# A two-block transformer kernel: second Fourier transform for 129 of 256 positions and the rest mirrored, one reciprocal per attention job, a double norm by one root

## What is computed

```python
def diff_attend(q, k, v, lam):
    s = jnp.einsum("bqhcd,bkhcd->bhcqk", q, k).astype(jnp.float32) * (HEAD_DIM ** -0.5)
    p = jax.nn.softmax(s, axis=-1)
    a = p[:, :, 0] - lam * p[:, :, 1]
    return jnp.einsum("bhqk,bkhe->bqhe", a.astype(v.dtype), v)

def fourier_mix(f):
    B, S = f.shape[:2]
    fg = f.reshape(B, S, N_FGROUPS, FGROUP_DIM).astype(jnp.float32)
    y = jnp.fft.fft2(fg, axes=(1, 3), norm="ortho").real
    return y.reshape(B, S, FOURIER_WIDTH).astype(f.dtype)

def rms_norm(x, g):
    xf = x.astype(jnp.float32)
    y = xf * lax.rsqrt(jnp.mean(xf * xf, axis=-1, keepdims=True) + EPS)
    return (y * g.astype(jnp.float32)).astype(x.dtype)
```

## Time and profile before

| | us |
|---|---|
| median of 3 runs | 2753.19 (2752.36 to 2753.29) |
| profiled execution, whole | 2750.1 |
| its span, first to last instruction | 2748.3 |
| TensorE busy | 2636.5 (96%) |
| VectorE busy | 1593.8 (58%) |
| ScalarE busy | 976.0 (36%) |
| mean granted TensorE clock | 0.977 of full |

### The profile page before, as it was taken

One profiled execution on the slowest core, in us unless ns is written; L12 is line 12 of the kernel. 1 busy time (PEld: TensorE's weight loads), 2 busy tenths in 40 slices (PEclk: granted clock), 3 DMA queues, 4 the chain that ended last, 5 costly groups with the idle time before them and its releaser, 6 DMA issues.

```text
span 2748.3 us, 36869 instructions
## 1 busy us (share of the span) xinstructions
PE 2636.5 (96%) x15140; PEld 2169.6 (79%) x15140; DVE 1593.8 (58%) x2895; ACT 976.0 (36%) x1737; POOL 52.5 (2%) x55
## 2 busy tenths in 40 slices
PE   8999999999999999999999999998998989997896
PEld 5888888867889888898888897898997777784442
DVE  4877765285447768558776473766555754444111
ACT  4322233276334222242222343744444523222111
POOL 0000000000000000000000000000000000001220
PEclk9999999999999999999999999999999899998998
DMA  7536452200323455334566332053525122157997
GB/s 312 204 141 245 151 195 90 108 1 31 123 92 123 159 202 198 131 123 169 213 269 252 136 123 92 32 209 125 211 85 204 47 77 93 62 222 312 401 382 301
DMA packets 56823, 456.53 MB, mean 166 GB/s; under 512 B 10704, under 2 KB 21328, under 8 KB 21840
## 3 DMA queue, kind: packets, MB, share of 16 engines
q1 hardware_dynamic: 49456, 446.01, 42.1%
q0 software_dynamic: 6912, 6.32, 0.7%
q10 hardware_dynamic: 288, 1.84, 0.2%
HBM read 497.11 MB, written 1.05 MB: 181 GB/s over the span
## 4 chain that ended last, share of the span: by engine, by line
PE 86%; DMA 5%; DVE 4%; ACT 2%; issue 1%; SPq 0%; POOL 0%; DVEq 0%; ACTq 0%; POOLq 0%
PE ps L516 65%; PE ps L2537 3%; PE ps L1926 3%; PE ps L1421 1%; PE ps L3517 1%; PE ps L3144 1%; PE ps L1398 1%; PE ps L2596 1%; PE ps L521 1%; DMA BIG<-eup 1%; DMA U<-edn 1%; DMA U<-eup,extra_ids 1%; ACT fh L503 1%; PE ps L3543 1%; PE nb L3543 1%
## 5 line engine op out<-in xcount | busy, mean ns | idle before, releaser
L516 PE MATMUL ps<-UL,fh 128*128 128x512 f32 (+1 forms) x2096 | 732.5, 349 | 11.4 <-DVE UL L867 5.3
L510 DVE TENSOR_TENSOR fl<-wr,fh 128x1024 fp32r<-128x1024 f32 (+2 forms) x436 | 481.9, 1107 | 446.5 <-ACT fh L503 445.7
L516 PE MATMUL ps<-UH,fl 128*128 128x512 f32 (+1 forms) x2096 | 729.8, 348 | 0.0
L516 PE MATMUL ps<-UH,fh 128*128 128x512 f32 (+1 forms) x2096 | 729.6, 348 | 0.0
L503 ACT CAST fh<-wr 128x1024 fp32r<-128x1024 f32 (+2 forms) x436 | 414.3, 954 | 319.3 <-PE ps L516 298.5
L516 PEld LDWEIGHTS ps<-UL,fh 128*128 128x128 f32 x2096 | 398.3, 190 | 65.3 <-DVE UL L867 6.0
L516 PEld LDWEIGHTS ps<-UH,fl 128*128 128x128 f32 x2096 | 398.5, 190 | 49.5
L516 PEld LDWEIGHTS ps<-UH,fh 128*128 128x128 f32 x2096 | 398.3, 190 | 49.6
L564 DVE SCALAR_TENSOR_TENSOR acc<-wr,CA 128x1024 f32<-128x1024 f32 x256 | 312.4, 1220 | 3.7
L516 PE MATMUL ps<-HL,fh 128*128 128x512 f32 (+1 forms) x770 | 267.4, 347 | 0.0
L516 PE MATMUL ps<-HH,fl 128*128 128x512 f32 (+1 forms) x770 | 266.9, 347 | 0.0
(11 more groups left out here) (565 smaller groups left out, 3542.2 us busy)
## 6 DMA issues: line engine op xcount, KB each, us to landing
wr<-ws SPq DMA_DIRECT2D x135, 2048.0 KB, 8.0
wr<-ws SPq DMA_DIRECT2D x32, 1408.0 KB, 5.9
wr<-eup SPq DMA_DIRECT2D x32, 1024.0 KB, 11.5
BIG<-eup SPq DMA_DIRECT2D x22, 1024.0 KB, 16.2
wr<-edn SPq DMA_DIRECT2D x16, 1024.0 KB, 14.2
wr<-ws SPq DMA_DIRECT2D x11, 1024.0 KB, 7.6
BIG<-edn SPq DMA_DIRECT2D x11, 1024.0 KB, 11.4
X<-eup SPq DMA_DIRECT2D x6, 1024.0 KB, 9.8
```

The source lines that it names most:

```text
L510: e.tensor_tensor(lv, raw_tile(sp.units[n]), hv.bitcast(F32), ALU.subtract).then_inc(*low_done.inc("low", event))
L516: i = e.matmul(out, l, r, start=first and n == 0, stop=last and n == len(pairs) - 1, skip_group_check=True)
```

## The change

In the loops: the transform over positions is made for 129 of 256 positions, the cosine part in the left half of NB and the sine part in the right half. With real output the position 256 − s has the same cosine part as s and the opposite sine part. ScalarE copies the cosine part of 129 positions ("fr even"); VectorE then writes the difference to positions 129 to 255, in reversed order, and the sum to positions 0 to 128 (`mirrored`). It does so at the start of every even job from the third on, and once behind the loop. The event "fr" is now VectorE's.

The two reciprocals of a job (two values for each query block) become one over four values, ahead of both blocks and behind the last exponential of the job. The product with minus lambda is taken into the scaling, as its second scalar.

Where the blocks meet: the sums of squares of both norms are made by matmuls with all-ones matrices, which leave them on every partition, and the factor of the second norm over the first is formed as one inverse root of (sum of the gained squares / D + eps × sum of squares / D + eps²). The inverse roots are a logarithm and an exponential over 256 columns. The root of the first norm, needed for the first block's output, is made by ScalarE behind the eight u.

```diff
@@ -777,13 +777,6 @@
-        def pe_spread(e, name, n, src):
-            e.wait_ge(*at("rms", name))
...
+        def pe_pair_means(e, name, prev):
+            e.wait_ge(*at("scaled", prev[:3], 7))
+            e.wait_ge(*at("square sum", prev, 6))
+            small = eps[:, 0:1].to_broadcast([128, 128])
+            e.matmul(NB[:, 256:512], ones, RS[:, 256:512], start=True, stop=False, skip_group_check=True)
+            e.matmul(NB[:, 256:512], small, RS[:, 0:256], start=False, stop=False, skip_group_check=True)
+            e.wait_ge(*at("square", prev, 7))
+            last = rot.of("stats", prev)
+            e.matmul(NB[:, 256:512], ones, last[:, 256:512], start=False, stop=False, skip_group_check=True)
+            e.matmul(NB[:, 256:512], small, last[:, 0:256], start=False, stop=True, skip_group_check=True).then_inc(
+                *sums.inc("pair sums", name))
+            e.wait_ge(*at("spread", name))
+            e.matmul(NB[:, 0:256], ones, RS[:, 0:256], start=True, stop=False, skip_group_check=True)
+            e.matmul(NB[:, 0:256], ones, last[:, 0:256], start=False, stop=True, skip_group_check=True).then_inc(
+                *sums.inc("stats", prev))
+
         def act_norm_pair(e, name, prev, shift):
-            e.wait_ge(*at("stats", prev))
-            e.activation(root[:, 0:2], NB[:, 0:2], ACT.Sqrt, scale=1.0 / D, bias=eps[:, :]).then_inc(*act.inc("first root", name))
-            e.wait_ge(*at("second square", name))
-            e.activation(root[:, 2:4], root[:, 2:4], ACT.Sqrt, scale=1.0 / D, bias=eps[:, :]).then_inc(*act.inc("root", name))
+            e.wait_ge(*at("pair sums", name))
+            e.wait_ge(*at("eps squared"))
+            e.activation(NB[:, 256:512], NB[:, 256:512], ACT.Ln, scale=1.0 / D, bias=st[:, 57:58]).then_inc(*act.inc())
+            e.wait_ge(*act.now())
+            e.activation(RS[:, 256:512], NB[:, 256:512], ACT.Exp, scale=-0.5).then_inc(*act.inc("spread", name))
             for k in range(8):
                 e.wait_ge(*at("scaled", name, k))
                 e.activation(U[:, k, 0:256], U[:, k, 0:256], ACT.Identity, bias=shift[:, 0, k:k + 1],
                              scale=AB[:, 0, k:k + 1]).then_inc(*act.inc("u", name, k))
+            e.wait_ge(*at("stats", prev))
+            e.activation(NB[:, 0:256], NB[:, 0:256], ACT.Ln, scale=1.0 / D, bias=eps[:, :]).then_inc(*act.inc())
+            e.wait_ge(*act.now())
+            e.activation(NB[:, 0:256], NB[:, 0:256], ACT.Exp, scale=-0.5).then_inc(*act.inc("first spread", name))
 
         def dve_norm_pair(e, name, first_gain, gain, scale):
             dve_gains(e, LAT, gain, scale)
             e.wait_ge(*dve.now())
             e.tensor_tensor(AB[:, 0, :], AB[:, 0, :], first_gain, ALU.mult).then_inc(*dve.inc())
-            e.wait_ge(*at("first root", name))
-            e.reciprocal(rinv[:, 0:2], root[:, 0:2]).then_inc(*dve.inc())
-            e.wait_ge(*dve.now())
-            e.tensor_tensor(root[:, 2:4], NB[:, 2:4], rinv[:, 0:2], ALU.mult).then_inc(*dve.inc())
-            e.wait_ge(*dve.now())
-            e.tensor_tensor(root[:, 2:4], root[:, 2:4], rinv[:, 0:2], ALU.mult).then_inc(*dve.inc("second square", name))
-            e.wait_ge(*at("root", name))
-            e.reciprocal(rinv[:, 2:4], root[:, 2:4]).then_inc(*dve.inc())
-            e.wait_ge(*dve.now())
-            e.tensor_tensor(rinv[:, 2:4], rinv[:, 2:4], rinv[:, 0:2], ALU.mult).then_inc(*dve.inc("rms", name))
             e.wait_ge(*at("spread", name))
             for k in range(8):
-                e.tensor_tensor(U[:, k, 0:256], X[:, k, 0:256], NB[:, 256:512], ALU.mult).then_inc(*dve.inc("scaled", name, k))
+                e.tensor_tensor(U[:, k, 0:256], X[:, k, 0:256], RS[:, 256:512], ALU.mult).then_inc(*dve.inc("scaled", name, k))
 
         def dve_first_block_out(e, first_gain, i):
 
+            if i == 0:
+                e.wait_ge(*at("first spread", "nmix"))
             for k in (2 * i, 2 * i + 1):
...
                 if half:
-                    (act_log_exp if halves else act_root_table)(e)
+                    act_log_exp(e)
...
                     e.wait_ge(*at("f1", l, s, g))
-                    for n, (l_, r_) in enumerate([(r[:, 0:128], cs[:, 0, :]), (r[:, 128:256], ss[:, 0, :]),
-                                                  (r[:, 256:384], cs[:, 1, :]), (r[:, 384:512], ss[:, 1, :])]):
-                        m = e.matmul(NB[:, 0:256], l_, r_, start=n == 0, stop=n == 3, skip_group_check=True)
+                    for x, table in enumerate((cs, ss)):
+                        for tt in range(2):
+                            m = e.matmul(NB[:, 256 * x:256 * x + 129], r[:, 256 * tt + 128 * x:256 * tt + 128 * x + 128],
+                                         table[:, tt, 0:129], start=tt == 0, stop=tt == 1, skip_group_check=True)
                     m.then_inc(*sums.inc("dft2", l, s, g))
...
-                        e.copy(frT[g][:, s * 256:s * 256 + 256], NB[:, 0:256]).then_inc(*act.inc("fr", l, s, g))
+                        e.copy(frT[g][:, s * 256:s * 256 + 129], NB[:, 0:129]).then_inc(*act.inc("fr even", l, s, g))
...
+            def mirrored(i):
+                s, g = divmod(i, 4)
+                f = frT[g][:, s * 256:s * 256 + 256]
+                e.wait_ge(*at("fr even", l, s, g))
+                e.tensor_tensor(f[:, 129:256][:, ::-1], f[:, 1:128], NB[:, 257:384], ALU.subtract).then_inc(*dve.inc())
+                e.wait_ge(*dve.now())
+                e.tensor_tensor(f[:, 0:129], f[:, 0:129], NB[:, 256:385], ALU.add).then_inc(*dve.inc("fr", l, s, g))
+
             for n, (h, s) in enumerate(jobs):
                 if n == len(jobs) - 1:
                     low_parts(e, sp, sp.next_one())
+                if n % 2 == 0 and 0 < n <= 8 * len(segs):
+                    mirrored(n // 2 - 1)
                 klo, khi = keys_of(s)
                 nk = khi - klo
                 for qb in range(2):
@@ -1738,18 +1755,20 @@
                         e.wait_ge(*at("score", l, n, qb, c))
                         e.tensor_reduce(st[:, z + c:z + c + 1], psum.of("p", l, n, qb, c)[:, 0:nk], AX.X, ALU.min).then_inc(
                             *dve.inc("least", l, n, qb, c))
+                zs_ = st[:, 16 + (n % 2) * 16:32 + (n % 2) * 16].rearrange("p (q x) -> p q x", q=2)
+                e.wait_ge(*at("p", l, n, 1, 1))
+                e.reciprocal(zs_[:, :, 2:4], zs_[:, :, 4:6]).then_inc(*dve.inc())
                 for qb in range(2):
                     z = 16 + (n % 2) * 16 + qb * 8
                     p0, p1 = PA[(n % 3) * 2 + qb], PA[6 + qb]
-                    e.wait_ge(*at("p", l, n, qb, 1))
-                    e.reciprocal(st[:, z + 2:z + 4], st[:, z + 4:z + 6]).then_inc(*dve.inc())
-                    e.wait_ge(*dve.now())
-                    e.tensor_tensor(st[:, z + 6:z + 7], st[:, z + 3:z + 4], nlam, ALU.mult).then_inc(*dve.inc())
-                    e.wait_ge(*dve.now())
-                    e.tensor_scalar(p1[:, 0:nk], p1[:, 0:nk], st[:, z + 6:z + 7], None, ALU.mult).then_inc(*dve.inc())
+                    if qb == 0:
+                        e.wait_ge(*dve.now())
+                    e.tensor_scalar(p1[:, 0:nk], p1[:, 0:nk], st[:, z + 3:z + 4], nlam, ALU.mult, ALU.mult).then_inc(*dve.inc())
                     e.wait_ge(*dve.now())
                     e.scalar_tensor_tensor(out=p0[:, 0:nk], in0=p0[:, 0:nk], scalar=st[:, z + 2:z + 3], in1=p1[:, 0:nk],
                                            op0=ALU.mult, op1=ALU.add).then_inc(*dve.inc("a", l, n, qb))
+            if len(jobs) == 8 * len(segs):
+                mirrored(4 * len(segs) - 1)
...
-            pe_stats(e, prev, 512, ("ffn", 1, 1))
-            pe_spread(e, "nmix", 4, rinv)
+            pe_pair_means(e, "nmix", prev)
...
-            e.wait_ge(*at("x", ("ffn", 1, 1, 1), 7))
+            e.memset(st[:, 57:58], EPS * EPS).then_inc(*dve.inc("eps squared"))
```

More of the change, by code:

```diff
@@ L778, in act_inverse_root @@
             e.activation(NB[:, 0:T], NB[:, 0:T], ACT.Exp, scale=-0.5).then_inc(*act.inc("spread", name))
-        def pe_spread(e, name, n, src):
-            e.wait_ge(*at("rms", name))
-            for t in range(n):
-                i = e.matmul(NB[:, t * 128:t * 128 + 128], src[:, t:t + 1].to_broadcast([128, 128]), ident, start=True,
-                             stop=True, skip_group_check=True)
-            i.then_inc(*sums.inc("spread", name))
         def dve_gains(e, segs, gain, scale, ks=slice(0, 8)):
```

## The result

The changed kernel takes 2762.42 us in the median of nine runs (2759.35 to 2767.32); nine runs of the kernel before beside them lie between 2744.06 and 2754.73 around 2753.19. The ratio is 1.0044, with an interval of 1.0033 to 1.0056: slower by 0.44% (the two medians are 9.2 us apart), where 0.57% had been forecast. The profiled execution has a span of 2760.6 us against 2748.3.

What follows compares the result with a forecast made beforehand. TensorE (9.78 us per pair) and a VectorE chain through ScalarE's exponentials bound the loop closely together. 11.45 + 4.1 + 0 = +15.6 us on 2750.1 gave 2765.7, plus 3.1 to the median: 2768.8, range 2762 to 2777.

Steps and rivals of the forecast that it cites:

- One reciprocal per job: Attention loops: joint reciprocal waits for block 2's last exponential; jobs become 6.29 us (512 keys) and 4.36 us (256).
- The mirror: VectorE, ahead of the even job's minima: two additions from PSUM add 0.53 us, bounds 0.45 and 0.72.
- The second scalar: VectorE's attention scaling: a second scalar read from memory adds 0.06 us to each scaling.
- the doubled rate: Rival, attention scaling: a second scalar in memory ends its doubled rate, adding 10.7 us, to 2779.5; chance 7%.
- The transform: Second position transform on TensorE: 129 columns cut it from 1.89 to 1.05 us, relieving 0.84 us per pair.
- First layer's shift: First attention loop: 78.59 us becomes 90.04, +11.45 us, passed on whole to what follows.
- Second layer: Second attention loop: 48.09 us becomes 53.04, +4.95, partly absorbed by TensorE at the end, leaving +4.1 us.
- Double norm: Where the blocks meet: 0 us, since a weight transfer releases TensorE; clock bounds −2.1 and +2.1 us.
- TensorE stays the bound: Rival, loops: VectorE's work fits under TensorE's 8.94 us per pair; 9 us faster, 2744; chance 4%.
- The clock falls: Rival, loops: TensorE's clock falls in thin stretches; once in each of eight pairs +8 us, 2777; chance 12%.
- About the same: Rival, loops: part of the wait overlaps unseen, giving 2748 to 2758 us; chance 6%.
- What would show it: Loop signs: pairs of 11.2 us, second-layer jobs of 6.3, VectorE gaps of 1.2 and some 1 us, scaling 0.55.

Runs made afterwards that it cites:

- The moved wait alone: Kernel before with only VectorE's wait for block 1's exponential put ahead of both query blocks: 2766.52 us, ratio 1.0062.
- the split alone: Kernel after with each query block given its own reciprocal again, behind its own exponential; transform, mirror, second scalar and norm stay: 2738.99 us, ratio 0.9953.
- the second-scalar kernel: Kernel before with only the product with minus lambda taken into the scaling as second scalar, two reciprocals kept: 2745.42 us, ratio 0.9975.
- six old-norm executions: Profiled runs with the old double norm, among them before and after with old norm (2764.98 us): 16.5 us mean from memset to end of gate rows.
- five executions: Profiled runs with the new double norm and the gate weights' load in its old place: 13.2 us mean from memset to end of gate rows.
- The two sets: Kernel after measured twice against the kernel before: 2762.42 us, ratio 1.0044, and again 2758.43 us, ratio 1.0028.
- the one with the joint reciprocal: Kernel before with only the attention reciprocal joined and the product with minus lambda taken into the scaling: 2758.79 us, ratio 1.0036.

## Why the prediction was right, point by point

**One reciprocal per job.** Right in mechanism and size. 3.60 us to the reciprocal of a 512-key job, measured 3.59; jobs of 6.29 and 4.36, measured 6.30 and 4.39; a pair of 11.18, measured 11.21. The moved wait alone reproduces the gaps, and the split alone removes them.

**The mirror** took 0.52 (0.53 forecast), the reversed write at 279 ns no more than a plain one. **The second scalar** costs 0.06 us, as forecast (0.55 and 0.41 us, where the earlier trace rows has 0.49 and 0.35), and the doubled rate is kept: that rival is out. **The transform** went from 1.89 to 1.05 us, as the earlier trace rows had it.

**First layer's shift.** From the first minimum to the last combination 90.22 (90.04 forecast); the gate tile stands at 648.80, 93.95 behind the loop's start at 554.85, where it was 82.45: +11.5. The start of the second loop follows the first by 1156.86 us instead of 1145.37, again +11.5. It was passed on whole.

**Second layer.** To the last combination 52.95 (53.04 forecast). TensorE's last gate-tile work, by the start of ScalarE's first root behind it, is 61.02 behind the loop's start where it was 57.05: +4.0 (+4.1 forecast). The reading that TensorE bounds the jobs of this loop before (it stands in the first rival, which gives four transforms a gain there, and in two expectations) was wrong, as the second-scalar kernel showed; it did not enter the sum, which took the loop's measured length.

**Double norm: the step that failed.** "I take 0", with a lower bound of −2.1 for the clock alone. The prediction read one chain of waits, saw the transfer last, and costed the norm's own chain at nothing because it was covered. But the cover was a tie: in before the norm would have let the gate rows start 6.9 us behind the memset (ScalarE's first u starts at 6.2, and where the norm came last the gate rows start 0.75 us behind that), the transfer at 7.9. In four of the six old-norm executions the order is the other way. And the second round of the old norm's small matmuls already ran at half clock, behind 1.6 us without TensorE work; with the new norm the clock stayed up (stretches, before and after):

```profile
2072.40:2074.48 2.08, 2.08 (x8) 1.78 (x8) 0.00 (x0) 0.00 (x0) 0.00 (x0) 0.50 1.09 378
```

```profile
2083.30:2085.00 1.70, 0.75 (x5) 0.32 (x3) 0.09 (x1) 0.83 (x2) 0.00 (x0) 1.00 0.99 369
```

Measured over five executions the new norm saves 3.3 us; in the profiled execution 4.5, of which 2.1 in the gate rows' clock, my lower bound, and 2.4 in their start.

**The sum.** 2768.8 was forecast and 2762.42 measured: inside the range of 2762 to 2777 by 0.4 us, and 0.4 below the forecast's own 2762.8 to 2773.2. The loops were right to 0.2 us; that the total stayed in the range is in part luck.

15.6 − 3.3 = 12.3 us. The two sets gave 0.44% and 0.28% of some 2752 us: 12.1 and 7.7. The first fits the corrected sum, the second lies 4.6 below, and its interval ends at 10.7. What is left is open.

The two profiled executions differ by 12.3 us in their spans, and that agreement is no proof either: the first loop starts 1.6 us earlier, the two loops' starts are 11.5 further apart, the second block's memset follows 3.2 later, and from there to the end only 0.7 us of the norm's 4.5 is left (679.5 before, 678.8 after). Over the same six and five executions as above that last distance has means of 679.6 and 675.9, so the saving does reach the end in the mean.

One source of such differences can be seen: two executions of the very same program took 666.0 and 659.8 us from the gate rows to the end, with different stretches of half clock. In each of these stretches of 30 us (the first of the kernel after, the second of its repetition, both from 65 us behind the gate rows) the granted clock differs:

```profile
2160.00:2190.00 30.00, 30.00 (x116) 25.62 (x116) 20.38 (x53) 17.69 (x55) 3.51 (x1) 0.58 0.00 1
```

```profile
2160.60:2190.60 30.00, 30.00 (x125) 25.88 (x125) 22.29 (x58) 17.99 (x55) 3.51 (x1) 0.64 0.00 1
```

**The rivals.** *TensorE stays the bound*: out, by its deciding point; the fourth sum is read 3.56 us behind the minima's start, not 2.40. The Trainium skill ("VectorE: DVE Perf Modes", Rules for kernel authors) asks to minimize the count of chained operations, not their semaphores. The kernel with only the second scalar follows that rule and gains 0.25%; the one with the joint reciprocal follows it too and loses 0.36%, because the joined instruction also joins two waits on another engine, and that the rule doesn't weigh. *The clock falls*: it did, within loop 1 (granted 0.95 from 554.8 to 648.8 in the kernel after, 1.00 in the earlier trace rows), yet loop 1 isn't longer for it: TensorE's slack took it up whole. I had priced such a fall at 1 us. *About the same*: out.

**What would show it.** The steady pairs, the gaps and the scaling are there as named. "TensorE busy for about 80% of a pair" is not: the row of a pair gives 11.07 of 11.21.

```profile
599.62:610.83 11.21, 11.07 (x53) 7.50 (x52) 8.78 (x22) 7.41 (x24) 0.00 (x0) 1.00 0.00 0
```

Its matmuls hold waits in their recorded length: in TensorE's order of time the eight score instructions of a 256-key job stand with 2.70 us, where they took 1.13 in before. Slack of TensorE must be read from whose wait ends last, not from its busy share.

## What to carry to other kernels

Before two small instructions are joined, ask what each one waits for. The joined one waits for the later, and everything behind it on its engine does too; here three steps of 0.19 us saved per job cost 1.1 us of exponentials that had run beside them. And where a chain of waits names one releaser, look how far behind the next one stands: a cover of one microsecond in one execution is a tie, and both ends have to be priced.

## What was not expected of the hardware

The stretch where the blocks meet ran at a granted clock of 0.57 to 0.72 in all six executions with many small matmuls and waits between them, and at 1.00 in six of seven with fewer and longer ones (0.86 in the seventh). A transfer of 1 MB at the same place took 5.5 to 7.6 us in the first kind and 5.0 to 5.4 in the five of the second that issue it there; why it is quicker there isn't settled. And falls of the clock that left 0.95 granted over the first loop cost it nothing where VectorE was the bound by 2 us per pair; in the second loop a fall came with 2.3 us in a single job where TensorE had the whole transform.
